# Down weights of each expert turn but the first, issued from ScalarE's queue instead of SyncE's

## The chip, the cores and the metric

The kernel runs on one core of one Trainium2 chip. The metric is the device time in microseconds of one execution. A second number used below is the span of the profiled execution, from its first to its last instruction, which is a little shorter than the time of that same execution.

## What is computed

The program is one inference step of a decoder layer on 288 tokens (256 of a prompt, 32 of eight sample sequences), model width 2048, everything in fp32. The change lies in the last stage, a mixture of 16 experts with a hidden width of 512. Each token goes to two experts:

```python
a = jnp.einsum('td,edf->tef', t, w_gate_e)      # 2048 -> 512, per expert
u = jnp.einsum('td,edf->tef', t, w_up_e)        # 2048 -> 512
hid = jax.nn.silu(a) * u * combine[..., None]
return jnp.einsum('tef,efd->td', hid, w_down_e) # 512 -> 2048
```

Only the chosen experts have a weight other than 0 in `combine`, so the kernel computes just those pairs. The three matrices of one expert are 4 MB each, 12 MB together, and each is read once or, if an expert has more than 64 tokens, once for each 64.

## The kernel before, in words

**Turns.** The expert stage is a loop of turns. A turn handles up to 64 tokens of one expert; here there are 16 turns, numbered 0 to 15, run as one pair ahead of a loop and seven pairs in a hardware loop. `wtab` holds the number of pairs in column 0 and the expert of turn t in column 2 + t.

**Pieces.** An expert's weights come in six transfers of 2 MB, called pieces n = 0 to 5: 0 is the first half of gate, 1 the first half of up, 2 the second half of gate, 3 the second half of up, 4 and 5 the two halves of down. A piece is 128 partitions by 16 KB. Below, 3(13) is piece 3 of turn 13.

**Slots.** The tile `ring` has six slots. Pieces 3, 4 and 5 of every turn go to the same three slots. Pieces 0 to 2 go to the other three in even turns and to three spare places (in `z`, `z` and `hT`) in odd turns. So pieces 0, 1 and 2 of turn t + 2 can be loaded once turn t has used its own, while 3, 4 and 5 of turn t + 1 must wait for turn t.

**Who issues.** All weights are issued by SyncE (SP) in program order, by `expert(e, pair, odd, first, last_n, back)` (L501 to L515). Each transfer first waits for a semaphore (L505 to L509) that TensorE increments when the last matmul on the slot is done, and `expert_of` (L517 to L519) reads the expert's number into a register. The order in the loop (L529 to L533) is: 0, 1, 2 of an even turn; 3, 4, 5 of the odd turn before it; 0, 1, 2 of the next odd turn; 3, 4, 5 of the even turn. L534 issues 3, 4, 5 of the last turn. The gathers of token rows are issued by GpSimd (L685 to L703), one per turn, 128 rows of 4 KB.

**TensorE's turn** (`two_turns`, L1270 to L1314): the first half of gate and up needs pieces 0 and 1 (64 instructions for both halves, two per call); the second half needs 2 and 3; then the next tokens are turned, `hid` is turned, and down half 0 (piece 4) and half 1 (piece 5) follow. In an even turn but the first, TensorE also does the eight pairs of `combine` matmuls (L1254 to L1263) for the two turns before it, between the gate and up matmuls, so an even turn is longer than an odd one.

**ScalarE's turn** (`two_turns`, L1530 to L1544): it waits for the last gate and up matmul, computes a sigmoid (L1536), copies the next tokens from PSUM to `hs` (`copy_rows`, L1517 to L1523, 16 instructions), waits for both down halves (L1541, L1542) and copies half of the turn's output rows from PSUM to `y_two` (L1543). VectorE copies the other half. All activations are recorded at line 1363, all matmuls at L712, transposes at L722, and all weight transfers at L515.

Of the kernel before, what the change touches and what calls it, by code (L numbers as in the profile page):

```python
# [17 lines left out]
P = 128  # L18
# [13 lines left out]
NE = NG * EG  # L32
# [9 lines left out]
SLOTS = 6  # L42
SLOT = 4096
# [25 lines left out]
def ds(i, n):  # L69
    return bass.ds(i, n)  # L70

def build(nc, io, out):
    with ExitStack() as ctx:
        made = {}

        def sem(name):

            if name not in made:
                made[name] = ctx.enter_context(nc.semaphore(name))  # L80
            return made[name]
# [17 lines left out]
        def sb(name, shape, dt=F32):  # L99
            return ctx.enter_context(nc.sbuf_tensor(name, shape, dt))  # L100
# [23 lines left out]
        wtab = sb("wtab", [1, 2 + NWIN], I32)  # L124
# [11 lines left out]
        def slot(s):  # L136
            return ring[:, (s % SLOTS) * SLOT:(s % SLOTS + 1) * SLOT]
# [56 lines left out]
        def state_of(b):  # L194

            first, _, o = states[(0, 0, 0, 0, 1, 1, 2, 2)[b]]
            return o[:, (b - first) * 1024:(b - first + 1) * 1024].rearrange("p (h v) -> p h v", h=H_A)
# [87 lines left out]
        spare = (z[:, 3072:3072 + SLOT], z[:, 7168:7168 + SLOT], hflat[:, 0:SLOT])  # L285
# [9 lines left out]
        MOE = WOUT + 8  # L295
# [3 lines left out]
        def place(n):  # L299

            later = LATER if n >= UP and n % SLOTS < 2 else 0
            return n // SLOTS - (1 if n % SLOTS < 2 else 0) + later

        def freed(n):

            return place(n) + 1 + (EXTRA + lead(n % SLOTS) if n >= UP and n % SLOTS < 4 else 0)

        def lead(s):

            return 1 if s in (2, 3) else 0  # L310
# [8 lines left out]
        def used(n, turn):  # L319

            return sem(f"ring_free{n % SLOTS}"), turn + (freed(n) + 1)

        def spared(n, odd):

            return odd and n < len(spare)

        def weights_at(n, odd):

            return spare[n] if spared(n, odd) else slot(MOE + n)

        def weights_full(n, pair, odd):

            if spared(n, odd):
                return sem(f"spare_full{n}"), pair * 16 + 16
            return sem(f"ring_full{(MOE + n) % SLOTS}"), (pair if n < len(spare) else pair * 2 + odd) * 16 + filled(MOE + n)
# [5 lines left out]
        def weights_read(n, pair, odd):  # L341

            if spared(n, odd):
                return sem(f"spare_free{n}"), pair + 2
            return used(MOE + n, pair if n < len(spare) else pair * 2 + odd)
# [5 lines left out]
        section_end = [min(G for G in range(48) if sum(late_pieces[:G + 1]) >= (i + 1) * KT) for i in range(4)]  # L351

        def ada_use(p):

            return ada_slots[:p].count(ada_slots[p])
# [9 lines left out]
        def _(sp):  # L366
# [18 lines left out]
            for p, s in enumerate(ada_slots):  # L385
                m, q = p // 4, p % 4
                at = (1 - m % 2) * D + m // 2 * 1024
                sp.wait_ge(sem(f"ring_free{s}"), ada_use(p) + 1)
                sp.dma_start(slot(s).rearrange("p (k n) -> p k n", k=4),
                             io["w_ada"][0, q * 4 * P:(q + 1) * 4 * P, at:at + 1024].rearrange("(k p) n -> p k n", p=P)).then_inc(sem(f"ring_full{s}"), 16)  # L390
                if p == 7:
                    first_win_load(0)
                if p == 10:
                    first_win_load(2)
# [98 lines left out]
            for n in range(8):  # L493
                j, q = n // 2, n % 2
                sp.wait_ge(sem(f"ring_free{(WOUT + n) % SLOTS}"), freed(WOUT + n))
                src = io["w_out"][0, q * 8 * P:(q + 1) * 8 * P, j * 512:(j + 1) * 512]
# [4 lines left out]
            def expert(e, pair, odd, first, last_n, back=0):  # L501

                for n in range(first, last_n):
                    if spared(n, odd):
                        sp.wait_ge(sem(f"spare_free{n}"), pair + 1)  # L505
                    elif n < len(spare):
                        sp.wait_ge(sem(f"ring_free{(MOE + n) % SLOTS}"), pair + freed(MOE + n))
                    else:
                        sp.wait_ge(sem(f"ring_free{(MOE + n) % SLOTS}"), pair * 2 + (odd - back + freed(MOE + n)))  # L509
                    sp.sem_inc(sem("seen"), 1)  # L510
                    if n < 4:
                        src = io[("w_gate_e", "w_up_e")[n % 2]][0, ds(e, 1)].rearrange("a (p k) n -> p (a k n)", p=P)[:, n // 2 * SLOT:(n // 2 + 1) * SLOT]
                    else:
                        src = io["w_down_e"][0, ds(e, 1)].rearrange("a (p k) n -> p (a k n)", p=P)[:, (n - 4) * SLOT:(n - 3) * SLOT]
                    sp.dma_start(weights_at(n, odd), src).then_inc(weights_full(n, 0, odd)[0], 16)  # L515

            def expert_of(at):  # L517

                return sp.value_load(wtab[0:1, ds(at, 1)], min_val=0, max_val=NE - 1)  # L519

            expert(0, 0, 0, 0, 6)
            sp.wait_ge(sem("htok_turned"), 4 * NT)
            sp.wait_ge(sem("h_stored"), 16 * NT)
# [4 lines left out]
            pairs = sp.value_load(wtab[0:1, 0:1], min_val=NE // 2, max_val=NWIN // 2 - 1)  # L528
            with sp.Fori(1, pairs) as pair:  # L529
                expert(expert_of(pair * 2 + 2), pair, 0, 0, len(spare))  # L530
                expert(expert_of(pair * 2 + 1), pair, 1, len(spare), 6, 2)
                expert(expert_of(pair * 2 + 3), pair, 1, 0, len(spare))
                expert(expert_of(pair * 2 + 2), pair, 0, len(spare), 6)  # L533
            expert(expert_of(pairs * 2 + 1), pairs, 1, len(spare), 6, 2)  # L534

            for c in range(NT):
                last = max(n for n in range(4 * NT) if parts[n][0] == c)
# [2 lines left out]
                n = min(TT, TP - c * TT)  # L540
# [169 lines left out]
        def _(pe):  # L710
# [67 lines left out]
            for p, s in enumerate(ada_slots):  # L778
                m, q = p // 4, p % 4
                pe.wait_ge(sem(f"ring_full{s}"), 16 * (ada_use(p) + 1))  # L780
                if q == 0 and m:
                    pe.wait_ge(sem("mod_row_ready"), m)
                w = slot(s).rearrange("p (k n) -> p k n", k=4)
                for r in range(2):
                    for kh in range(2):
                        for c in range(2):
                            g = 32 * (2 * kh + c)
                            last = mm(ps[g:g + 32, 7, :], cT[:, 4 * q + 2 * kh + r, :], w[:, 2 * kh + r, c * 512:(c + 1) * 512],
                                      q == 0 and r == 0, q == 3 and r == 1)
                if q < 3:  # L790
                    last.then_inc(sem(f"ring_free{s}"), 1)
                else:
                    last.then_inc(sem("mod_summed"), 1)
                    release("mod_summed", m + 1, s)
                if q == 3:
                    turn_half(m)
                early_products({7: 4, 8: 6, 9: 6, 10: 14, 11: 4, 12: 6, 13: 6, 14: 6}.get(p, 0))
# [563 lines left out]
        def _(act):  # L1361
            def f(o, i, func, **kw):
                return nc.scalar.activation(o, i, func, **kw)  # L1363
# [93 lines left out]
            for h in range(H_B):  # L1457
# [3 lines left out]
                for q in range(2):  # L1461
                    lo, n = q * P, P * (q + 1)
# [46 lines left out]
            for n in range(12):  # L1509
                if n in (6, 9):  # L1510
                    e = rt[:, 400:412] if n == 6 else rt[:, 420:423]
# [5 lines left out]
            def copy_rows(n, first=0):  # L1517
                act.wait_ge(sem("hs_turned"), n)
                for a in range(first, 2):
                    for i in range(8):  # L1520
                        k = 4 * a + i // 2 + 8 * (i % 2)
                        last = f(hs[:, k, :], ps[:, 1 + a, i * W:(i + 1) * W], ACT.Identity, bias=shift_pk[:, k:k + 1])
                last.then_inc(sem("hs_ready"), 1)  # L1523
# [5 lines left out]
            pairs = act.value_load(wtab[0:1, 0:1], min_val=NE // 2, max_val=NWIN // 2 - 1)  # L1529
            def two_turns(pair, first):  # L1530

                for half_turn in range(2):
                    it = pair * 2 + half_turn
                    act.wait_ge(*weights_read(2, pair, half_turn))
                    act.wait_ge(*weights_read(3, pair, half_turn))
                    f(sg, ps[0:W, 0, :], ACT.Sigmoid).then_inc(sem("sg_ready"), 1)  # L1536
                    copy_rows(it + 2)
                    rows = slice(half_turn * W, (half_turn + 1) * W)
                    if half_turn == 0 and not first:
                        act.wait_ge(sem("combined"), pair * 8 + 8)  # L1540
                    act.wait_ge(*used(MOE + 4, it))  # L1541
                    act.wait_ge(*used(MOE + 5, it))  # L1542
                    f(y_two[rows, half_turn * 1024:(half_turn + 1) * 1024].rearrange("p (a n) -> p a n", a=2), ps[rows, 4:6, :],  # L1543
                      ACT.Copy).then_inc(sem("y_copied_too"), 1)  # L1544
# [773 lines left out]
```

## Time and profile before

| what | us |
|---|---|
| median of 3 runs | 1856.55 |
| the runs | 1850.34 to 1860.96 |
| the profiled execution's own time | 1859.33 |
| its span | 1857.8 |
| TensorE busy over the span | 1717.1 (92%) |
| ScalarE busy over the span | 242.6 (13%) |
| queue q1 (SyncE's), share of the 16 DMA engines over the span | 60.2% |
| queue q10 (ScalarE's), the same | 0.5% |

How to read it: a busy share over the whole span mixes stages with different limits, and the change touches only the expert stage, from about 1345 us to 1828 us of the span. TensorE's busy time counts overlapping matmuls once. For a single stage one reads a view cut to it. A DMA has two times: the issue, when the queue's engine hands it out, and the landing, when its semaphore is complete; the difference holds its own transfer and everything that was ahead of it on the DMA engines.

### The profile page before, as it was taken

Reading aid. Unit: us, or ns where it says so; the run is one execution under the profiler, and the core shown is the slowest. Engines: PE = TensorE matmul, PEld = TensorE weight load, DVE = VectorE, ACT = ScalarE, POOL = GpSimd, SP = SyncE. Lnnn points to the kernel's source line nnn. Section 1 sums busy time; section 2 is a strip of 40 time slices with the busy share of each in tenths; the row PEclk is TensorE's granted clock in tenths of the full one; section 3 lists DMA queues with packets and bytes.
Section 4 is the critical chain, followed back from the end, with each engine's and each line's share of the span. In section 5 each row is a group of like instructions: output and inputs, shape, how many; then the busy total and the mean of one; then the engine's idle time right before and its main releaser. Section 6 shows DMA issues by size and latency. Waiting matters only on the chain.

```text
span 1857.8 us, 27829 instructions
## 1 busy us (share of the span) xinstructions
PE 1717.1 (92%) x10995; PEld 1083.4 (58%) x10995; DVE 526.8 (28%) x1164; ACT 242.6 (13%) x619; POOL 153.7 (8%) x274
## 2 busy tenths in 40 slices
PE   7899999999999999996888999999689989999997
PEld 4466666666667786764666777777533333333334
DVE  3110000000018754456555121111313223332233
ACT  2010000000001200211222200000221111111113
POOL 1001111111112000240000000000010000000000
PEclk9899999999999999997999999999799999999999
DMA  9999877776624433646999795333599999999981
GB/s 338 398 382 343 301 261 295 283 274 250 247 92 152 155 104 116 229 180 225 354 392 391 293 355 206 95 148 124 211 410 426 428 428 428 428 428 427 428 359 51
DMA packets 157868, 531.13 MB, mean 286 GB/s; under 512 B 19909, under 2 KB 64107, under 8 KB 136187
## 3 DMA queue, kind: packets, MB, share of 16 engines
q1 hardware_dynamic: 128834, 432.24, 60.2%
q0 software_dynamic: 18176, 97.15, 14.0%
q10 hardware_dynamic: 10786, 0.75, 0.5%
q8 instruction: 50, 0.82, 0.2%
q14 instruction: 22, 0.18, 0.0%
HBM read 510.95 MB, written 19.15 MB: 285 GB/s over the span
## 4 chain that ended last, share of the span: by engine, by line
PE 66%; DMA 12%; issue 12%; SPq 3%; DVE 3%; POOL 1%; DVEq 1%; POOLq 1%; ACT 1%; ACTq 0%
PE ps L712 63%; DMA ring<-in_w_up_e_dram 6%; PE ps L722 3%; DMA xT<-in_w_ada_dram 2%; DMA xT<-in_w_in_dram 2%; DMA ring<-in_w_ada_dram 1%; SPq L437 1%; SPq L431 1%; POOL work L592 1%; POOLq L591 1%; DVE ring L1954 0%; DVE work L1571 0%; DVEq L2260 0%; DVE work L1580 0%; DMA ring<-in_cache_k_dram 0%
## 5 line engine op out<-in xcount | busy, mean ns | idle before, releaser
L712 PE MATMUL ps<-hT,ring 128*128 128x288 f32 x2304 | 586.9, 411 | 4.8 <-PE ps L712 3.3
L712 PEld LDWEIGHTS ps<-hT,ring 128*128 128x128 f32 x2304 | 430.3, 190 | 168.4 <-issue 56.8
L712 PE MATMUL ps<-ring,work 128*64 128x512 f32 (+1 forms) x1408 | 335.5, 626 | 14.6 <-DVE work L1580 6.6
L712 PE MATMUL ps<-z,ring 128*128 128x288 f32 (+1 forms) x1040 | 257.2, 409 | 4.5 <-PE ps L712 2.7
L712 PEld LDWEIGHTS ps<-z,ring 128*128 128x128 f32 x1040 | 197.5, 191 | 63.4 <-issue 6.6
L1580 DVE COPY z<-ps 128x288 f32<-128x288 f32 (+5 forms) x70 | 47.6, 686 | 535.2 <-PE ps L712 526.4
L712 PEld LDWEIGHTS ps<-ring,work 128*64 128x64 f32 (+1 forms) x1408 | 97.1, 136 | 174.0 <-issue 160.8
L1577 DVE SCALAR_TENSOR_TENSOR xT<-ps,modT,xT 128x256 f32<-128x256 f32 x144 | 63.7, 479 | 183.4 <-PE ps L712 183.3
L1363 ACT ACTIVATE z<-ps 128x512 f32<-128x512 f32 (+3 forms) x79 | 44.0, 607 | 517.0 <-PE ps L712 513.1
L1363 ACT ACTIVATE work<-ps 128x288 f32<-128x288 f32 (+2 forms) x57 | 27.7, 486 | 601.9 <-PE ps L712 601.9
L712 PE MATMUL ps<-work,z 128*128 128x288 f32 (+3 forms) x418 | 87.3, 372 | 10.8 <-DVEq L2203 7.3
L712 PE MATMUL ps<-hT,xT 128*128 128x288 f32 x256 | 75.4, 460 | 23.4 <-DMA xT<-in_w_in_dram 23.4
L712 PE MATMUL ps<-ring,z 32*32 32x256 f32 (+2 forms) x3232 | 82.7, 356 | 10.4 <-DVE ring L1954 8.7
L712 PE MATMUL ps<-z,work 128*32 128x512 f32 (+1 forms) x512 | 89.1, 597 | 3.2 <-DMA z<-in_w_ada_dram 1.8
L722 PE MATMUL ps<-ident,z 128*128 128x128 f32 (+3 forms) x444 | 66.3, 293 | 22.9 <-DVE z L1571 11.8
L712 PEld LDWEIGHTS ps<-work,z 128*128 128x128 f32 (+3 forms) x418 | 50.3, 163 | 57.4 <-DVEq L2240 32.3
L712 PEld LDWEIGHTS ps<-ring,z 32*32 32x32 f32 (+2 forms) x3232 | 67.9, 108 | 25.7 <-issue 18.7
L712 PEld LDWEIGHTS ps<-hT,xT 128*128 128x128 f32 x256 | 55.1, 218 | 41.9 <-DMA xT<-in_w_in_dram 25.1
L722 PEld LDWEIGHTS ps<-ident,z 128*128 128x128 f32 (+3 forms) x444 | 50.2, 147 | 48.5 <-issue 32.6
L1954 DVE STREAM_TRANSPOSE ring<-ring 128x2048 f32<-128x2048 f32 x32 | 72.4, 2294 | 6.6 <-issue 3.5
L712 PE MATMUL ps<-hT,work 128*64 128x512 f32 (+1 forms) x192 | 63.1, 542 | 10.5 <-DMA ring<-in_w_up_e_dram 10.1
L1580 DVE COPY work<-ps 64x512 f32<-64x512 f32 (+5 forms) x37 | 21.1, 572 | 161.2 <-PE ps L712 149.1
(236 smaller groups left out, 1001.3 us busy)
## 6 DMA issues: line engine op xcount, KB each, us to landing
ring<-in_w_in_dram SPq DMA_DIRECT2D x36, 2048.0 KB, 14.2
ring<-in_w_down_e_dram SPq DMA_DIRECT2D x32, 2048.0 KB, 18.1
ring<-in_w_up_e_dram SPq DMA_DIRECT2D x24, 2048.0 KB, 19.4
ring<-in_w_ada_dram SPq DMA_DIRECT2D x16, 2048.0 KB, 16.9
z<-in_w_ada_dram POOLq DMA_DIRECT2D x32, 1024.0 KB, 7.8
xT<-in_w_ada_dram POOLq DMA_DIRECT2D x32, 1024.0 KB, 7.0
ring<-in_cache_v_dram SPq DMA_DIRECT2D x64, 512.0 KB, 5.8
ring<-in_cache_k_dram SPq DMA_DIRECT2D x64, 512.0 KB, 5.9
```

Of the source, the lines that this page charges most:

```text
L431: pg = sp.value_load(ptab[0:1, ds(b * NPG + (s % 2 * 4 + n), 1)], min_val=0, max_val=io["cache_k"].shape[1] - 1)
L437: sp.dma_start(slot(s)[:, n * 1024:(n + 1) * 1024], io[name][0, ds(pg, 1)].rearrange("a p h d -> (a p) (h d)")).then_inc(sem(f"kv_full{s}" ...
L591: pg = pool.value_load(ptab[0:1, ds(i * 2 * NPG + k, 1)], min_val=0, max_val=io["cache_k"].shape[1] - 1)
L592: pool.dma_start(lf_in[:, ds(i * 2 + k // NPG, 1), k % NPG, :].rearrange("p a h -> p (a h)"), io["cache_logf"][0, ds(pg, 1)].rearrange("a ...
L712: return nc.tensor.matmul(o, lhsT, rhs, start=start, stop=stop, skip_group_check=free)
L722: return nc.tensor.transpose(o, i, ident[0:n, 0:n])
L1363: return nc.scalar.activation(o, i, func, **kw)
L1577: return nc.vector.scalar_tensor_tensor(out=o, in0=a, scalar=s, in1=b, op0=op0, op1=op1)
L1580: return nc.vector.tensor_copy(o, a)
L1954: nc.vector.transpose(kT[:, g, 4 * half:4 * half + 4], slot(half).rearrange("p (n g e) -> p n g e", n=4, g=2)[:, :, g]).then_inc(sem("keys ...
```

## The change

ScalarE issues pieces 4 and 5 of turns 1 to 15 on its own queue, at the head of its turn, that is right behind the copy of the preceding turn's outputs in its program. SyncE issues pieces 4 and 5 of turn 0 only. The waits are on the same semaphores and values as before. ScalarE reads the expert's number from `wtab` itself.

```diff
+        def down_half(e, n):
+
+            return io["w_down_e"][0, ds(e, 1)].rearrange("a (p k) n -> p (a k n)", p=P)[:, (n - 4) * SLOT:(n - 3) * SLOT]
+
...
                     else:
-                        src = io["w_down_e"][0, ds(e, 1)].rearrange("a (p k) n -> p (a k n)", p=P)[:, (n - 4) * SLOT:(n - 3) * SLOT]
+                        src = down_half(e, n)
...
             with sp.Fori(1, pairs) as pair:
                 expert(expert_of(pair * 2 + 2), pair, 0, 0, len(spare))
-                expert(expert_of(pair * 2 + 1), pair, 1, len(spare), 6, 2)
+                expert(expert_of(pair * 2 + 1), pair, 1, len(spare), 4, 2)
                 expert(expert_of(pair * 2 + 3), pair, 1, 0, len(spare))
-                expert(expert_of(pair * 2 + 2), pair, 0, len(spare), 6)
-            expert(expert_of(pairs * 2 + 1), pairs, 1, len(spare), 6, 2)
+                expert(expert_of(pair * 2 + 2), pair, 0, len(spare), 4)
+            expert(expert_of(pairs * 2 + 1), pairs, 1, len(spare), 4, 2)
...
                 for half_turn in range(2):
                     it = pair * 2 + half_turn
+                    if half_turn or not first:
+                        e = act.value_load(wtab[0:1, ds(it + 2, 1)], min_val=0, max_val=NE - 1)
+                        for n in (4, 5):
+                            s = (MOE + n) % SLOTS
+                            act.wait_ge(sem(f"ring_free{s}"), it + freed(MOE + n))
+                            act.dma_start(slot(MOE + n), down_half(e, n)).then_inc(sem(f"ring_full{s}"), 16)
                     act.wait_ge(*weights_read(2, pair, half_turn))
                     act.wait_ge(*weights_read(3, pair, half_turn))
```

## Rows read from the trace of the kernel before

**Rows 1.** Windows by stage: us, busy us (instructions), TensorE clock, DMA share, GB/s.

```profile
1330.00:1370.00 40.00, 24.91 (x108) 11.98 (x110) 10.01 (x39) 7.20 (x27) 7.01 (x6) 0.72 0.84 327
1370.00:1443.00 73.00, 68.21 (x302) 25.27 (x298) 19.40 (x47) 10.99 (x37) 2.29 (x4) 0.98 1.01 428
1688.70:1750.10 61.40, 57.00 (x250) 21.74 (x250) 18.17 (x46) 9.97 (x36) 2.29 (x4) 0.97 1.01 427
1750.10:1791.60 41.50, 39.32 (x166) 14.64 (x167) 11.75 (x32) 5.01 (x19) 1.15 (x2) 0.96 0.92 391
```

**Rows 2.** Waits of 1443 to 1791.6 us: total us, times, longest.

```profile
PE ps L712 <- DMA ring<-in_w_up_e_dram: 10.1, 6, 2.3
```

**Rows 3.** Chain that ended last, in order of time, from 1731 us: start, us, what.

```profile
1731.69 18.34 DMA ring<-in_w_up_e_dram
...
1750.08 7.14 PE ps L712 x32
...
1761.04 30.48 PE ps L712 x120
...
1794.80 22.04 PE ps L712 x100
...
1820.65 7.11 PE ps L712 x32
```

**Rows 4.** SyncE's timeline: start, us, issues. The first two are 3(9) and 3(11).

```profile
1609.04 0.33 SPq L515 DMA_DIRECT2D ring<-in_w_up_e_dram  x1
...
1670.39 0.33 SPq L515 DMA_DIRECT2D ring<-in_w_up_e_dram  x1
...
1719.54 0.34 SPq L515 DMA_DIRECT2D ring<-in_w_gate_e_dram  x1
1720.06 0.33 SPq L515 DMA_DIRECT2D ring<-in_w_up_e_dram  x1
1730.36 0.33 SPq L515 DMA_DIRECT2D ring<-in_w_gate_e_dram  x1
1731.69 0.33 SPq L515 DMA_DIRECT2D ring<-in_w_up_e_dram  x1
1738.52 3.69 SPq L515 DMA_DIRECT2D ring<-in_w_down_e_dram  x2
1748.82 0.33 SPq L515 DMA_DIRECT2D z<-in_w_gate_e_dram  x1
```

**Rows 5.** Issues in single windows: 3(14) at 1758.65, then 3(15) at 1791.76; last number is us to landing.

```profile
ring<-in_w_up_e_dram SPq DMA_DIRECT2D x1, 2048.0 KB, 22.0
...
ring<-in_w_up_e_dram SPq DMA_DIRECT2D x1, 2048.0 KB, 7.6
```

**Rows 6.** TensorE's timeline, turns 12 to 14: start, us, what, idle before.

```profile
1741.54 7.04 PE L712 MATMUL ps<-z,work 128*64 128x512 f32 x32
1750.08 0.64 PE L712 MATMUL ps<-hT,work 128*64 128x512 f32 x1 [1.50 <-DMA ring<-in_w_up_e_dram]
1761.04 10.50 PE L712 MATMUL ps<-ring,work 128*64 128x512 f32 x40 [0.80 <-DVE work L1580]
...
1780.57 1.24 PE L712 MATMUL ps<-work,z 128*128 128x288 f32 x4
1781.74 1.94 PE L712 MATMUL ps<-ring,work 128*64 128x512 f32 x8
```

**Rows 7.** ScalarE's timeline, turns 12 and 13, then the output copy of turn 13.

```profile
1730.23 0.59 ACT L1363 ACTIVATE work<-ps 64x512 f32<-64x512 f32 x1 [20.64 <-PE ps L712]
...
1741.82 1.02 ACT L1363 ACTIVATE z<-ps 64x1024 f32<-64x1024 f32 x1 [7.26 <-PE ps L712]
1757.28 0.59 ACT L1363 ACTIVATE work<-ps 64x512 f32<-64x512 f32 x1 [14.44 <-PE ps L712]
...
1769.92 1.02 ACT L1363 ACTIVATE z<-ps 64x1024 f32<-64x1024 f32 x1 [8.32 <-PE ps L712]
```

**Rows 8.** DMA of 1703 to 1709.2 us, one gather beside weights: packets, MB, share of 16 engines.

```profile
DMA packets 276, 2.61 MB, mean 420 GB/s; under 512 B 33, under 2 KB 33, under 8 KB 145
...
q1 hardware_dynamic: 148, 2.15, 81.5%
q0 software_dynamic: 128, 0.46, 18.4%
```

**Rows 9.** DMA of 1791 to 1794 us in 40 slices, GB/s: nothing moves until slice 24.

```profile
GB/s 0 0 0 0 0 0 0 0 0 0 0 0 0 0 0 0 0 0 0 0 0 0 0 874 874 437 655 218 0 0 0 0 218 0 218 0 0 0 218 218
```

## The prediction

> **What bounds the kernel now.** I read the windows by stage first. From 1370 us to about 1780 us the DMA engines have a share of 1.01 and move 427 or 428 GB/s in every window, and TensorE is busy for 57.0 of each 61.4 us [rows 1]. So the expert stage is paced by its weights: a pair of turns brings twelve pieces and two gathers, and 3(9), 3(11) and 3(13) are issued 61.35 and 61.30 us apart [rows 4]. A pair moves 12 x 2.097 + 2 x 0.524 = 26.2 MB, which at 427 GB/s is 61.4 us: the bytes alone are the period. One piece is 4.9 us of all engines. Second, who waits: TensorE waits for a DMA six times, 10.1 us in all, always for piece 3 of an odd turn [rows 2]. It is a close race: without that 1.5 us a pair TensorE would need 59.8. Third, the chain that ended last: its last link that is a DMA is 3(13), issued at 1731.69 and landing 18.34 us later, at 1750.03; from there TensorE runs without a DMA wait to the end of the stage [rows 3]. So the end moves with the resumption of TensorE at 1750.08, unless a later piece becomes late.
>
> **What is removed and added.** SyncE loses 30 issues, ScalarE gets them, with 15 register loads. SyncE costs nothing either way: its order did not hold back the pieces behind down. 5(13) was issued at 1738.52 + 3.69 - 0.33 = 1741.88, and the next, 0(15), at 1748.82, when the first half of turn 13's matmuls (7.04 us from 1741.54) ended [rows 4, 6]; it waited for TensorE and still will. On ScalarE, a register load costs about 0.8 us by SyncE's rows (1730.36 to 1731.69 with one between, against 1719.54 to 1720.06 without) and an issue 0.33 [rows 4]: 1.5 us a turn. Behind them waits only the sigmoid, before which ScalarE is idle for 14.4 to 20.6 us [rows 7]. Cost nothing; only if an issue took over 6 us each would the sigmoid be late. The added waits are on semaphores that the output copy has waited for already, so they are free too.
>
> **When down is now issued.** SyncE issued 4(13) at 1738.52 and 5(13) at 1741.88. ScalarE's copy starts at 1741.82 and takes 1.02 [rows 7]; with 0.8 for the register, 4(13) is issued at 1743.6, 5.1 us later than before, and 5(13) at about 1744.1, 2.2 later. Transfers start some 1.0 us after issue: with the engines idle, 3(15), issued at 1791.76, has its first bytes in slice 24 of 40 in 3 us, at 1792.7 [rows 9]. So down starts at 1744.6. For turn 14 the same steps from 1769.92 give 1772.7 [rows 7].
>
> **What that does to piece 3.** Before, everything was in one queue: down stood behind 3(t) and could not delay it. Now two queues share 16 engines that are full. How they share is read where it already happens: while a gather on q0 runs beside weights on q1, 6.2 us hold 276 packets, 33 of them mere markers; the gather's 0.46 MB are 112 rows of 4 KB and the weights' 2.15 MB are 131 of 16 KB [rows 8]. So engines take about one row from each in turn. Down and gate/up have equal rows of 16 KB, so while both wait each gets half.
>
> In an odd turn, 3(13) has 4.8 us of transfer left when down starts (landing 1750.03, less some 0.6 for its semaphore, less 1744.6): shared, it lands 4.8 us later. In an even turn 3(14) was issued at 1758.65 and took 22.0 us, to 1780.65 [rows 5]; TensorE needed it at 1781.74 [rows 6], so it had 1.1 us of cover. At 1772.7 some 7.3 us of bytes up to it are left, so it lands 7.3 us later and TensorE would wait 6.2.
>
> These are first-time costs. Once TensorE is behind by y, it copies later, so down starts y later and overtakes y less. Call y_o the lag of TensorE against before when it resumes at piece 3 of an odd turn, y_e the same in an even turn. An even turn gives y_e = 7.3 - 1.1 - y_o, or y_o if that is more. An odd turn had 1.5 us of wait that a lag can eat: y_o = y_e - 1.5, or 4.8 - y_e if that is more. Both hold at y_e = 3.8, y_o = 2.4 (then 4.8 - 3.8 = 1.0 is less than 2.4, so the odd wait disappears). The same bytes still take 61.35 us a pair: the wait of 1.5 a pair moves from piece 3 of odd turns to piece 3 of even turns, and is not repeated on top. What the end sees is the lag after turn 14: **+3.8 us**. I take it between the ends 0 (the engines keep to order of issue, nothing is overtaken) and 6.2 (no lag before the last even turn), since it is where the two conditions meet.
>
> **The clock.** After the odd wait TensorE's clock falls for a moment: down of turn 13 with eight more takes 10.50 us for 40, some 8.7 for 32, where turn 15, which had no wait, takes 7.11 [rows 3, 6]. The mean of 0.97 [rows 1] holds this. If the odd wait goes and the clock stays at its upper level, 1.65 us a pair are saved on TensorE and returned at once as a longer even wait, since the DMA sets the pace; with TensorE 1.65 sooner at the copy, y_e = 7.3 - 1.1 + 1.65 - y_o, and the lag is 4.7. It stays in the range.
>
> **The end.** Down of turn 15 is now issued at about 1803.2 + 1.0 + 0.8 + 3.8 = 1808.8 (turn 14's copy follows its down matmuls, which end near 1803), and two pieces need 7.6 + 4.9 us on idle engines [rows 5]: 1821.3. TensorE needs piece 4 at 1820.65 + 3.8 = 1824.4 [rows 3]. Cover 3 us and more, cost nothing.
>
> **Sum.** +3.8 on the profiled execution's 1859.33 gives 1863.1. That execution lies 2.8 above the median of the three runs, so I predict 1856.55 + 3.8 = 1860.3. A measurement of this kernel can tell about 0.5%, 9.3 us, from no change; 3.8 is 0.2%.
>
> **Rivals.**
> (a) *The DMA queues run dry behind piece 3 of odd turns* (slower). Before, down was queued 5 us ahead of need and bridged the gap to 0(15). Now the queue holds only what is left of 3(13) when down starts: 4.8 us less the lag of 3.8, a cushion of 1.0. From there on each further us between copy and first byte is lost bandwidth, and the bandwidth is the pace, in each of seven pairs. If ScalarE needs 3 us more than I read from SyncE's rows, that is 7 x 2.0 + 3.8 = +17.8: 1874. For it: the cushion is that thin. Against: the lag is no more than it needs to be, and a dry stretch shortens it. Chance 0.19.
> (b) *Down is served wholly before gate and up.* Piece 3 of an odd turn then lands up to 9.8 us late. If TensorE waited that long in each pair beside its own 59.8, a pair would take 69.6 for 61.3, and six of them up to 6 x 8.3 = +50: 1906. Against: the even sharing with the gather [rows 8]. The rows of the gather show one for one. Chance 0.05.
> (c) *Freed from the down waits, SyncE issues the rest sooner and TensorE's waits vanish* (faster): at most 10.1 us [rows 2], 1846.5. Against: rows 4 and 6 show SyncE waiting for TensorE, not behind down, and engines that are full from 1370 us on [rows 1] can't bring 3(13) sooner unless something ahead of it is put back; nothing is. Chance 0.04.
> (d) *Nothing moves*, because the engines serve by order of issue, or the later start of down spares piece 3: 0 to +1, 1857. Chance 0.12.
> The forecast has 0.60.
>
> **How the numbers follow.** The range takes the forecast and (d) with the spread of the runs (1850 to 1861) below, and most of (a) above: 1851 to 1876. Outside are (b), (c) and the end of (a). Slower by over 0.5% (above 1865.8): most of (a), (b), and a small part of the forecast at the 6.2 end: 0.23. Faster: (c) and the chance of the runs, 0.05. Same: 0.72.
>
> **What the profile after should show.** About 30 down issues on ScalarE's queue, 4(t) and 5(t) about 2 us behind each output copy; q10 with 63 MB. TensorE's DMA waits at piece 3 of even turns, 1 to 3 us each, and few or none at odd ones; down landing in 7 to 16 us instead of 16 to 20; piece 3 of turn 14 landing later against its need; windows of a pair still 61.3 to 61.4 us with a DMA share of 1.01. The end of down of turn 15 some 4 us later. I am wrong if the pair's period grows above 61.5 (then (a) or (b): the DMA share falls, or the odd waits reach 10 us), or if waits for DMA add up to less than before.

## The result, and the profile after

| | median us | runs | ratio to before | 95% interval |
|---|---|---|---|---|
| before | 1856.85 | 20 | | |
| changed | 1867.96 | 20 | 1.0053 | 1.0042 to 1.0065 |

The change costs 0.53%, 9.8 us (7.8 to 12.1 by the interval). One of the 20 runs took 2274 us and is not in the ratio. The medians of the table lie 11.1 us apart; differences below are taken from the ratios. The forecast was +3.8 us and "within 0.5%"; the time lies in the range of 1851 to 1876, the size is well over twice the forecast.

The windows by stage of the kernel after (us, busy us of TensorE, weight loads, VectorE, ScalarE and GpSimd, TensorE's clock, DMA share, GB/s) answer to [rows 1]:

```profile
1360.00:1424.00 64.00, 55.40 (x233) 20.27 (x234) 14.88 (x37) 9.35 (x35) 2.33 (x4) 0.95 1.01 428
1424.00:1487.30 63.30, 58.50 (x250) 22.43 (x251) 18.23 (x47) 10.01 (x37) 2.29 (x4) 0.95 0.99 414
...
1549.40:1610.60 61.20, 56.87 (x250) 21.84 (x250) 18.19 (x47) 9.97 (x36) 2.29 (x4) 0.97 1.00 421
1610.60:1675.90 65.30, 57.31 (x250) 22.00 (x250) 18.22 (x47) 10.02 (x37) 2.29 (x4) 0.95 0.99 420
1675.90:1735.50 59.60, 56.74 (x250) 21.80 (x249) 18.15 (x47) 9.96 (x37) 2.29 (x4) 0.97 0.98 409
```

The windows run from pair to pair. They are no longer equal, and the engines no longer move 427 GB/s in each. From 1380 to 1775 us the comparison is this, first the kernel before, then the one after:

```profile
1380.00:1775.00 395.00, 365.86 (x1594) 138.96 (x1591) 114.54 (x287) 64.80 (x234) 14.90 (x26) 0.97 1.01 427
```

```profile
1380.00:1775.00 395.00, 360.94 (x1564) 138.13 (x1561) 113.30 (x283) 64.81 (x234) 14.90 (x26) 0.96 0.99 418
```

A share of 0.99 for 1.01 over 395 us is 8 us of transfer time that was not used; 418 for 427 GB/s says the same.

TensorE's waits over the expert stage, after (total us, times, longest), against [rows 2], and each of them in TensorE's timeline:

```profile
PE ps L716 <- DMA ring<-in_w_up_e_dram: 18.3, 7, 5.1
```

```profile
1377.37 0.61 PE L716 MATMUL ps<-hT,work 128*64 128x512 f32 x1 [0.93 <-DMA ring<-in_w_up_e_dram]
1412.76 3.39 PE L716 MATMUL ps<-ring,work 128*64 128x512 f32 x8 [3.97 <-DMA ring<-in_w_up_e_dram]
1475.84 2.42 PE L716 MATMUL ps<-ring,work 128*64 128x512 f32 x8 [1.95 <-DMA ring<-in_w_up_e_dram]
...
1663.89 3.68 PE L716 MATMUL ps<-ring,work 128*64 128x512 f32 x8 [5.13 <-DMA ring<-in_w_up_e_dram]
...
1787.31 3.26 PE L716 MATMUL ps<-ring,work 128*64 128x512 f32 x8 [2.34 <-DMA ring<-in_w_up_e_dram]
```

The first is at turn 1. The other six read only `ring` weights, so they are even turns (2, 4, 6, 8, 10 and 14), each for piece 3. Before, all six were at odd turns, for `hT` and `ring` together [rows 6]. Behind a long wait TensorE also runs at its lower clock: the eight matmuls at 1663.89 take 3.68 us (granted clock 0.50), where eight without a wait take 1.94 (granted clock 1.00).

**Where the time went inside the stage.** ScalarE's output copies mark the turns. Their starts in turns 0, 2, 14 and 15, first before, then after:

```profile
1374.69 1.02 ACT L1363 ACTIVATE z<-ps 64x1024 f32<-64x1024 f32 x1 [6.33 <-PE ps L712]
...
1434.04 1.02 ACT L1363 ACTIVATE z<-ps 64x1024 f32<-64x1024 f32 x1 [7.26 <-PE ps L712]
...
1803.16 1.02 ACT L1363 ACTIVATE z<-ps 64x1024 f32<-64x1024 f32 x1 [7.26 <-PE ps L712]
1827.84 1.02 ACT L1363 ACTIVATE z<-ps 64x1024 f32<-64x1024 f32 x1 [6.62 <-PE ps L712]
```

```profile
1369.67 1.02 ACT L1367 ACTIVATE z<-ps 64x1024 f32<-64x1024 f32 x1 [6.33 <-PE ps L716]
...
1435.63 1.02 ACT L1367 ACTIVATE z<-ps 64x1024 f32<-64x1024 f32 x1 [7.26 <-PE ps L716]
...
1810.38 1.02 ACT L1367 ACTIVATE z<-ps 64x1024 f32<-64x1024 f32 x1 [7.25 <-PE ps L716]
1836.75 1.02 ACT L1367 ACTIVATE z<-ps 64x1024 f32<-64x1024 f32 x1 [8.31 <-PE ps L716]
```

| stretch | before | after | more |
|---|---|---|---|
| turn 0 to 2 | 59.35 | 65.96 | 6.6 |
| turn 2 to 14 (six pairs) | 369.12 | 374.75 | 5.6 |
| turn 14 to 15 | 24.68 | 26.37 | 1.7 |

Together 13.9 us in this pair of executions. The stage began 5.0 us earlier in the one after, with no change to the code ahead of it (among the kernels below the first copy starts anywhere from 1368.0 to 1375.5), so the spans differ by only 8.9.

So there are three parts: a loss in the first pair, 5.5 of its 6.6 us between the copies of turns 1 and 2; a pair that takes 62.46 instead of 61.52 us on average; and, at the end, a fall of TensorE's clock in the down matmuls of turn 15, which take 8.78 us against 7.11 [rows 3]. The third can't be put down to the change: the first experiment below shows it as well.

```profile
1827.87 8.78 PE L716 MATMUL ps<-ring,work 128*64 128x512 f32 x32 [0.79 <-DVE work L1590]
```

**How the engines share.** DMA of 1778 to 1782 us of the kernel after, when down of turn 14 (q10, ScalarE's) and 3(14) (q1, SyncE's) are in flight together:

```profile
DMA packets 108, 1.77 MB, mean 442 GB/s; under 512 B 0, under 2 KB 0, under 8 KB 0
...
q10 hardware_dynamic: 58, 0.95, 55.8%
q1 hardware_dynamic: 50, 0.82, 48.0%
```

Rows of equal size, near enough one for one, as [rows 8] had said. One row takes an engine about 0.6 us, and the engines turn from queue to queue nearly in step. So short windows at 1777.90 to 1778.15, 1778.50 to 1778.75 and 1779.10 to 1779.36 us show them change over row by row (shares are above 100% because a row lasts longer than the window):

```profile
q10 hardware_dynamic: 11, 0.18, 168.8%
```

```profile
q1 hardware_dynamic: 11, 0.18, 169.2%
```

```profile
q10 hardware_dynamic: 11, 0.18, 163.3%
```

**Where the engines run dry.** The chain around turn 10, SyncE's issues of 1(12) and 2(12), and the DMA of 1674 to 1679 us in 40 slices:

```profile
1637.28 26.57 DMA ring<-in_w_up_e_dram
1663.89 11.90 PE ps L716 x40
```

```profile
1658.35 0.33 SPq L519 DMA_DIRECT2D ring<-in_w_up_e_dram  x1
1675.98 0.33 SPq L519 DMA_DIRECT2D ring<-in_w_gate_e_dram  x1
```

```profile
GB/s 131 262 262 1180 262 131 262 131 262 0 0 0 131 0 0 0 0 131 0 0 0 0 0 524 524 524 0 393 0 131 131 131 0 131 524 393 655 131 0 786
```

3(10) takes 26.57 us to land. TensorE resumes at 1663.89, ends the second half near 1675.8, and only then can SyncE issue 2(12). By then everything else has been moved, down of turn 10 included, and for 1.7 us, until slice 24 at 1676.9, the engines carry next to nothing. A second, shorter kind of dry stretch lies behind piece 3 of an odd turn, just before down starts: 4(3) is issued at 1436.43, and nothing moves from 1437.0 to 1437.4. Piece 3 is late, so piece 2 and the next piece 3 are issued late, so the queues empty, and in a stage that is paced by bytes the lost bytes are not made up. These two stretches are some 2 of the 8 us; the others were not followed one by one.

### The profile page after: what moved, and what is told of

Same layout as the page of the kernel before. It is cut to its first block, busy times and chain, and to the rows that moved or that the text cites. A ratio compares the mean times of both kernels' runs of the same rounds, so it can differ in the third digit from the quotient of the medians.

```text
span 1866.7 us, 27854 instructions
## 1 busy us (share of the span) xinstructions
PE 1719.4 (92%) x10995; PEld 1083.7 (58%) x10995; DVE 526.1 (28%) x1164; ACT 242.3 (13%) x620; POOL 153.8 (8%) x274
## 4 chain that ended last, share of the span: by engine, by line
PE 63%; DMA 15%; issue 12%; SPq 3%; DVE 2%; DVEq 1%; POOL 1%; ACT 1%; POOLq 1%; ACTq 0%
PE ps L716 61%; DMA ring<-in_w_up_e_dram 9%; PE ps L726 2%; DMA xT<-in_w_in_dram 2%; DMA xT<-in_w_ada_dram 2%; DMA ring<-in_w_ada_dram 1%; SPq L441 1%; SPq L435 1%; POOL work L596 1%; POOLq L595 1%; DVEq L2250 0%; DVE ring L1964 0%; DVEq L2270 0%; POOL z L594 0%; DMA ring<-in_cache_k_dram 0%
## 5 line engine op out<-in xcount | busy, mean ns | idle before, releaser
L726 PE MATMUL ps<-ident,z 128*128 128x128 f32 (+3 forms) x444 | 66.3, 293 | 21.8 <-DVE z L1581 11.1
```

The costliest lines, as they stand in the source:

```text
L726: return nc.tensor.transpose(o, i, ident[0:n, 0:n])
```

## The experiments

They were run in three groups, each beside fresh runs of the kernel before. Theory O is order (down on its own queue passes ahead of piece 3), L is lateness alone, T is a cost of two active queues as such.

### Late issue, same queue

```diff
                         sp.wait_ge(sem(f"ring_free{(MOE + n) % SLOTS}"), pair * 2 + (odd - back + freed(MOE + n)))
+                        if n == 4 and not isinstance(pair, int):
+                            sp.wait_ge(sem("y_copied_too"), pair * 2 + (odd - back + 2))
```

> Down stays on SyncE's queue in the old order, but SyncE waits for ScalarE's output copy before piece 4 of each turn from 1 on, so that piece 4 is issued about 5 us later and piece 5 about 2 us later, as in the changed kernel. Theory O (order: on a queue of its own down passes ahead of piece 3 of the even turns, and the rest follows from that): nothing is passed and at least 4.8 us of piece 3 are still queued when down starts, so 0 to +1.5 us against before, TensorE's DMA waits still at odd turns, about 10 us in all, DMA share 1.01. Theory L (it is the later issue alone that costs): +8 to +10 us, DMA share 0.98 to 0.99. Theory T (two queues at once make the engines slower): 0.

Measured: 1856.83 us, ratio 0.9995 (0.9981 to 1.0009). 

Waits of TensorE in the expert stage:

```profile
PE ps L714 <- DMA ring<-in_w_up_e_dram: 9.9, 6, 2.5
```

Window of 1380 to 1775 us:

```profile
1380.00:1775.00 395.00, 366.09 (x1592) 139.32 (x1590) 116.05 (x292) 65.01 (x234) 14.94 (x26) 0.97 1.01 428
```

Down was issued behind the copy in this kernel too (SyncE issues 4(13) at 1739.00, the copy before it starts at 1737.77), and nothing changed. Theory L falls.

Its down matmuls of turn 15 are slow as well, though it loses nothing and its last DMA wait is in turn 13, as in the kernel before:

```profile
1816.56 8.44 PE L714 MATMUL ps<-ring,work 128*64 128x512 f32 x32 [0.80 <-DVE work L1582]
```

### Own queue, early issue

ScalarE's loop is cut so that it issues piece 4 ahead of the output copy and piece 5 behind it (`down_load` reads the expert, waits for the slot and issues; `front` is the sigmoid and `copy_rows`).

```diff
+                down_load(pair * 2, 4)
+                copy_y(pair - 1, 1, False)
+                down_load(pair * 2, 5)
+                front(pair, 0)
```

> Down on ScalarE's queue, but piece 4 issued as soon as down half 0 of the preceding turn is done (before the output copy, as early as SyncE did) and piece 5 right behind the copy. Theory O: down passes more of the queue, 3 of an even turn is first late by up to 9.8 us, so the waits of even turns grow while the dry stretches go: +8 to +14 us against before, DMA share back to 1.00 or 1.01. Theory L: the gap closes, 0 to +3 us. Theory T: as the changed kernel, about +10 us, with the share still below 1.

Measured: 1872.03 us, ratio 1.0085 (1.0057 to 1.0113), +15.8 us.

Waits of TensorE in the expert stage:

```profile
PE ps L716 <- DMA ring<-in_w_up_e_dram: 24.5, 8, 5.8
```

Window of 1380 to 1775 us:

```profile
1380.00:1775.00 395.00, 359.26 (x1570) 138.03 (x1572) 112.95 (x283) 64.66 (x234) 14.90 (x26) 0.97 0.99 419
```

Earlier down is worse, as O said and the reverse of L: it passes more. 15.8 us is a little more than the +8 to +14 that O gave. The interval is wide and just overlaps that of the changed kernel. But O's share of 1.00 or more is a miss: it stays at 0.99. So the dry stretches do not come from a late down alone; the late piece 3 makes them by itself, through TensorE, as at turn 10 above.

### Own queue for the odd turns only, for the even turns only

```diff
-                    if half_turn or not first:
+                    if half_turn == 1 and not (half_turn == 0 and first):
```

for the odd turns, `half_turn == 0` for the even ones, with the other parity's calls of `expert` on SyncE back to piece 6.

> ScalarE issues down of the odd turns only (behind the copy of an even turn), SyncE those of the even turns. Theory O: only 3 of the odd turns can be passed, by at most 4.8 us, and 1.5 us of wait absorbs part: +2 to +4 us, waits at odd turns, none at even ones. Theory L: half of the loss, +4 to +5 us. Theory T: +5 us, with half of the slower transfers.

Measured: 1857.68 us, ratio 1.0000 (0.9984 to 1.0017).

Waits of TensorE in the expert stage:

```profile
PE ps L716 <- DMA ring<-in_w_up_e_dram: 13.2, 4, 5.3
```

Window of 1380 to 1775 us:

```profile
1380.00:1775.00 395.00, 363.37 (x1594) 139.22 (x1596) 115.35 (x290) 65.02 (x234) 14.96 (x26) 0.97 1.01 427
```

> ScalarE issues down of the even turns only (behind the copy of an odd turn), SyncE those of the odd turns. Theory O: 3 of the even turns is passed by up to 7.3 us, with 1.1 us of cover: a first loss of 6.2 us, then a lag of 3.8 to 6.2; odd turns can't run dry since their down is queued early: +4 to +7 us, waits at even turns only. Theory L: +4 to +5 us. Theory T: +5 us.

Measured: 1866.10 us, ratio 1.0040 (1.0026 to 1.0054), +7.4 us.

Waits of TensorE in the expert stage:

```profile
PE ps L716 <- DMA ring<-in_w_up_e_dram: 18.0, 4, 6.5
```

Window of 1380 to 1775 us:

```profile
1380.00:1775.00 395.00, 362.91 (x1574) 138.75 (x1571) 115.73 (x291) 65.02 (x234) 14.94 (x26) 0.96 1.00 423
```

With odd turns only, the waits are at turns 1, 3, 7 and 11, up to 5.3 us long, yet no loss is measured (2 to 4 us had been expected by O; the interval ends at +3.2): the share is full, and the waits have moved and not added up. With even turns only, four waits at even turns and a share of 1.00 bring back about three quarters of the loss. Most of the loss lies in down of the even turns passing piece 3 of the even turns.

### Piece 3 ahead of piece 2: on the kernel before, and on the changed one

```diff
+                even, odd_before, odd = expert_of(pair * 2 + 2), expert_of(pair * 2 + 1), expert_of(pair * 2 + 3)
+                expert(even, pair, 0, 0, 2)
+                expert(odd_before, pair, 1, 3, 4, 2)
+                expert(even, pair, 0, 2, 3)
+                expert(odd_before, pair, 1, 4, 6, 2)
```

and the same for the other half of the pair; in the changed kernel without the calls for 4 to 6.

> The kernel before, all weights on SyncE, but piece 3 of turn t+1 is issued ahead of piece 2 of turn t+2, which is needed a turn later; both experts' numbers are read at the head of the pair. Theory O (what counts is where piece 3 stands in the order of transfers): 3 of an odd turn lands 4.9 us plus about 0.8 us of a register load sooner, the odd waits go or shrink, the period stays 61.3 us by the bytes and the end comes 3 to 6 us earlier than before. Rival B (the stage is bound by bytes from its first to its last transfer, so that order cannot matter): 0.

Measured: 1851.26 us, ratio 0.9966 (0.9949 to 0.9983), -6.3 us.

Waits of TensorE in the expert stage:

```profile
PE ps L717 <- DMA ring<-in_w_up_e_dram: 4.9, 2, 2.5
PE ps L717 <- DMA ring<-in_w_down_e_dram: 0.4, 1, 0.4
```

Window of 1380 to 1775 us:

```profile
1380.00:1775.00 395.00, 370.33 (x1618) 140.56 (x1616) 116.70 (x294) 65.02 (x234) 14.97 (x26) 0.97 1.01 427
```

The share cannot be better than before and is not; TensorE's DMA waits fall from 10.1 to 5.3 us. By ScalarE's output copies the gain is made once and not in each pair: turns 0 to 2 and 2 to 4 take 57.65 and 58.05 us for 59.35 and 62.12, turns 4 to 14 take 307.2 for 307.0. So order does count in a stage bound by bytes; that it does by how far TensorE is when the last byte lands is argued, not shown. It was run again:

> The kernel with piece 3 ahead of piece 2, all on SyncE, a second time on other runs: -6 us against before, -4 to -8, if the first result holds.

Measured: 1850.32 us, ratio 0.9957 (0.9943 to 0.9971), -8.0 us, with 7.2 us of DMA waits.

> The changed kernel (down on ScalarE's queue) with piece 3 issued ahead of piece 2 in the same way. Theory O: when down starts, only about 1.6 us of piece 3 of an even turn are left to be passed and its cover has grown by 5.7 us, so the loss of 9.8 us is gone: -4 to +2 us against before, DMA share 1.00 or 1.01, no wait at even turns. Theory T (two queues running at once cost engine time by themselves): +4 us or more, with the share still at 0.99.

Measured: 1858.10 us, ratio 1.0006 (0.9989 to 1.0023).

Waits of TensorE in the expert stage:

```profile
PE ps L719 <- DMA ring<-in_w_down_e_dram: 13.1, 6, 3.6
```

Window of 1380 to 1775 us:

```profile
1380.00:1775.00 395.00, 362.76 (x1577) 137.48 (x1574) 115.82 (x291) 65.03 (x234) 14.97 (x26) 0.97 1.01 428
```

Down is still on its own queue, and the loss is gone: share 1.01 again, no wait for piece 3. Theory T falls. But the gain of the order is not there either; TensorE now waits for down. In the chain of this kernel 5(13), issued at 1737.55, takes 23.04 us:

```profile
1737.55 23.04 DMA ring<-in_w_down_e_dram
```

### Is it the sharing or the lateness that makes down late there?

The kernel with piece 3 ahead of piece 2, all on SyncE, with the wait for `y_copied_too` of the first experiment.

> All weights on SyncE with piece 3 ahead of piece 2, and piece 4 held back until ScalarE's output copy. With down on ScalarE's queue the same order gave nothing against before, with TensorE waiting 13 us for down. If the equal sharing with pieces 0 and 1 of the next turn made down late (theory O), one queue keeps it on time: -4 to -7 us, hardly a wait for down. If its later issue made it late (theory L): -1 to +1 us, with 10 us or more of waits for down.

Measured: 1852.06 us, ratio 0.9971 (0.9957 to 0.9985), -5.4 us.

```profile
PE ps L719 <- DMA ring<-in_w_up_e_dram: 10.1, 5, 2.5
PE ps L719 <- DMA ring<-in_w_down_e_dram: 1.2, 3, 0.4
```

One queue, the same late issue, and 1.2 us of waits for down instead of 13.1. So it is the sharing: with a queue of its own down gets half the engines while it is the piece wanted next, and pieces 0, 1 of the next turns, not wanted for long, get the other half. The waits of this kernel add up to 11.3 us, more than the 10.1 before, and it still gains 5.4: their sum does not tell the time.

### All of 3, 4 and 5 on ScalarE's queue

```diff
+            def back(pair, half_turn, first, last=False):
+                it = pair * 2 + half_turn
+                if not last:
+                    load_on_act(it + 1, 3)
+                copy_rows(it + 2)
...
+                    load_on_act(it + 1, 4)
+                    load_on_act(it + 1, 5)
```

> ScalarE issues pieces 3, 4 and 5 of turns 1 to 15 (3 right behind the sigmoid of the turn before, 4 and 5 behind its output copy), SyncE only 0, 1 and 2. Theory O: down cannot pass piece 3, and piece 3 passes 0, 1 and 2 of later turns, which have 20 us and more of cover; it lands in 10 to 12 us instead of 18 to 22: -4 to -8 us against before, waits for piece 3 gone. Theory T: +4 us or more, since two queues are busy for most of the stage.

Measured: 1856.96 us, ratio 0.9992 (0.9978 to 1.0006). The waits for piece 3 went, as expected; the gain did not come.

```profile
PE ps L713 <- DMA ring<-in_w_down_e_dram: 12.6, 6, 3.2
```

Again it is down that TensorE waits for; that the shared engines bring it late is argued from the kernel above. The expectation had looked at piece 3 alone.

### Piece 3 ahead of 1 and 2

```diff
-                expert(even, pair, 0, 0, 2)
+                expert(even, pair, 0, 0, 1)
                 expert(odd_before, pair, 1, 3, 4, 2)
-                expert(even, pair, 0, 2, 3)
+                expert(even, pair, 0, 1, 3)
```

> All weights on SyncE, piece 3 of turn t+1 issued ahead of both 1 and 2 of turn t+2 (order 0, 3, 1, 2, then 4, 5). Theory O: 3 lands two pieces (9.8 us) sooner than in the kernel before, at 1740 where it landed at 1750; 1 and 2 have a turn of cover. What waits were left with one piece's advance (4.9 us) can go too, unless down becomes the piece that is waited for or the engines run dry before piece 3 (about 2 us of queue are left when it is issued): -5 to -10 us against before. Rival B (byte-bound from end to end): as with one piece's advance, -6.

Measured: 1853.07 us, ratio 0.9970 (0.9952 to 0.9989), -5.6 us: no more than with one piece's advance.

```profile
PE ps L717 <- DMA ring<-in_w_down_e_dram: 14.0, 8, 2.1
```

No wait for piece 3 is left; eight for down have taken their place. Pieces 1 and 2 now stand between 3 and 4 in the queue.

## Why the prediction was right or wrong

**What bounds the stage: right.** Bytes set the pair, and the last DMA in the chain is a piece 3 in both kernels. Of the kernels above, those whose share stayed at 1.01 lie between -8.0 and +1.1 us by their ratios; those whose share fell (the changed one, the early one, the even one) are the three that lost.

**ScalarE's and SyncE's work costs nothing: right.** ScalarE's shortest idle time before the sigmoid is 12.7 us, before and after. Its timeline around down of turns 13 and 14:

```profile
1747.05 1.02 ACT L1367 ACTIVATE z<-ps 64x1024 f32<-64x1024 f32 x1 [7.26 <-PE ps L716]
1747.83 0.85 ACTq L1543 DMA_DIRECT2D ring<-in_w_down_e_dram  x2
1760.79 0.59 ACT L1367 ACTIVATE work<-ps 64x512 f32<-64x512 f32 x1 [12.72 <-PE ps L716]
...
1773.09 1.02 ACT L1367 ACTIVATE z<-ps 64x1024 f32<-64x1024 f32 x1 [7.97 <-PE ps L716]
1774.18 0.85 ACTq L1543 DMA_DIRECT2D ring<-in_w_down_e_dram  x2
```

**When down starts: wrong, by two errors of opposite sign.** I took copy, then register, then issue, 1.8 us after the copy's start. It is 0.8 and 1.1. But the first byte 1.0 us after the issue holds only for idle engines [rows 9]. 4(14) is issued at 1774.18, and up to 1777.6 the engines carry rows of q1 alone: 3.4 us. Only where q1 had just run empty, as at 4(3), is it 1.0. So down of an even turn starts 4.5 us after the copy's start and not 2.8, and passes 1.7 us less than I reckoned. In the two equations of the prediction that makes a lag of 3.0 for 3.8: the forecast should have been smaller, and the miss is greater than it looks.

**The later issue itself is free: right**, by the first experiment. **Sharing row by row: right**, 58 against 50 rows.

**Waits move from odd to even turns: right**, with one at turn 1 besides. **The first-time loss of 6.2 us at an even turn: right in size, in part by luck.** Between the copies of turns 1 and 2 it is 5.5 us: 4.0 of wait and 1.5 because the eight matmuls behind it take 3.39 for 1.94 us at the lower clock. I had reckoned 6.2 of wait alone, from a down that I let start too early, and had charged no clock to even turns.

**The step that failed** is "The same bytes still take 61.35 us a pair", and with it the relaxing to a lag of 3.8. The term of 3.8 measured 13.9 in the profiled execution, 9.8 in the ratio. I had let the lag come back on its own because a later TensorE makes down pass less; but a later TensorE also makes SyncE issue pieces 2 and 3 later, and then the queues are empty. The forecast itself left a cushion of 1.0 us at the odd turns and put this into rival (a) at 0.19. That mechanism is what happened, in part and mostly elsewhere: ScalarE needed less time than I had read, not 3 us more, and the longest dry stretch is not behind piece 3 of an odd turn but behind the whole even turn. It took the pair from 61.5 to 62.5 us. By the prediction's own sign, a period above 61.5 with a fallen share, its forecast was wrong; the time lies in the range only because the range took in most of (a). That an empty queue is the cause of those 5.6 us is read from the share, the GB/s and the timeline, and from the two kernels in which order alone was put right; no run added an empty stretch by itself.

**The end: right on the wait.** Down of turn 15 made nobody wait. But its matmuls ran partly at the lower clock, 1.7 us, where I had charged the clock to odd turns with a wait. That is no cost of the change as far as is known: they take 8.4 to 8.8 us in seven of the twelve kernels profiled, one execution each, the first experiment among them, and 7.1 in the other five. What decides it stays open. The windows of the last stretch of the stage, before and then after, show the granted clock in the third column from the right:

```profile
1791.60:1827.90 36.30, 33.29 (x160) 13.03 (x158) 9.55 (x22) 8.99 (x36) 1.14 (x2) 1.00 0.47 188
```

```profile
1798.80:1836.80 38.00, 35.00 (x160) 13.46 (x159) 9.55 (x22) 8.99 (x36) 1.14 (x2) 0.96 0.45 179
```

**Rivals.** (b), whole pieces served first, falls by the row counts. For the same reason the figure of 9 to 17 descriptors that the Trainium skill gives (DMA: Bandwidth & Descriptors, queues, rings and completion order) does not describe these two queues: the trace shows them change over after every row. (c), SyncE freed, did not show. (d) fits the kernel with odd turns only, not the full change.

## What to carry to other kernels

In this stage, where the DMA engines are full, a second queue added no bandwidth (427 or 428 GB/s at most with one queue or two); it took the order of arrival out of the programmer's hands, and a transfer that was harmless behind the urgent one took half the engines from it. Before moving a load to another queue, list what is in flight at that moment and by how much each piece is early: here 1.1 us for 3(14), against 34 us for 2(15), issued just ahead of it (landed at 1757.4 + 18.4 = 1775.8, used at 1809.8). And look for gain in the order on the one queue: issuing the piece with the least cover one place sooner (0.9966 and 0.9957) beat both kernels.

## What was not expected of the hardware

ScalarE's DMA issue did not wait for the end of the copy in front of it: the copy of turn 12 starts at 1747.05 and takes 1.02 us, and the issue starts at 1747.83, although the register load lies between them. And TensorE's clock did not fall only where it had waited in the same turn: the down matmuls of turn 15, a turn without a DMA wait in both kernels, took 8.78 us in one and 7.11 in the other, at a mean clock of 0.96 and 1.00 over the stretch. The last wait was in turn 14 after and in turn 13 before, but that is not the reason by itself: in the first experiment's kernel the last wait was in turn 13 too, and they took 8.44. Last, a transfer's first row came 1.0 us after its issue on idle engines, and 3.4 us after it on full ones, though on a queue of its own with nothing ahead of it.
